# Reordering the input-projection units of a two-layer hybrid encoder: convolution units between query, key and value units

## The reference

```
h = rms_norm(x); q_a,k_a,v_a, q_r,k_r,v_r,g_r, z,xbc,dt = split(h @ w_in)
ya = sliding-window attention with sinks      (8 heads, 2 KV heads, 128 keys, relative bias)
yr = retention: rotary q,k; decayed scores; state carried over chunks; group norm; silu(g_r) *
ys = Mamba-2 SSD: xbc = silu(causal_dwconv(xbc)); decayed scores and states; * silu(z); group norm
x  = x + concat(ya, yr, ys) @ w_out
u  = rms_norm(x) @ w_up; a,b = halves;  x = x + (silu(causal_dwconv(a)) * b) @ w_down
```

## Time and profile before

| | |
|---|---|
| median of 3 runs | 1386.2 us (1384.06 to 1390.82) |
| span of the profiled execution | 1380.0 us |
| time around the span, taken as median less span | 6.2 us |
| PE busy | 1343.3 us, 97% of the span |
| DVE, ACT, POOL busy | 656.8, 628.5, 575.6 us |

### The profile page before, as it was taken

The page is one execution under the profiler, slowest core; times in us unless marked ns, Lnnn a source line. Parts: engine busy times, 40 slices in busy tenths (PEclk is TensorE's granted clock), DMA queues, the critical chain, the costliest instruction groups (busy, mean ns, idle before and its releaser), DMA issues.

```text
span 1380.0 us, 21798 instructions
## 1 busy us (share of the span) xinstructions
PE 1343.3 (97%) x6226; PEld 1071.1 (78%) x6226; DVE 656.8 (48%) x935; ACT 628.5 (46%) x965; POOL 575.6 (42%) x433
## 2 busy tenths in 40 slices
PE   6999999999999999999999999999999999999995
PEld 4787777778888888888877777777778888888884
DVE  7864567456444203443276555763754440144423
ACT  6431267166766423333362223743676662233333
POOL 3433334144554444554444333332544445444443
PEclk9999999999999999999999999999999999999998
DMA  6322122123333332333322221221323333333332
GB/s 194 100 62 62 53 70 77 39 69 92 93 105 100 99 99 84 95 103 94 106 78 76 62 62 52 59 76 45 100 78 105 98 91 107 93 90 100 98 94 105
DMA packets 65656, 119.47 MB, mean 87 GB/s; under 512 B 7320, under 2 KB 8632, under 8 KB 65464
## 3 DMA queue, kind: packets, MB, share of 16 engines
q1 hardware_dynamic: 65592, 118.64, 29.8%
HBM read 116.12 MB, written 2.49 MB: 86 GB/s over the span
## 4 chain that ended last, share of the span: by engine, by line
PE 82%; DVE 10%; issue 4%; ACT 3%; DVEq 0%; DMA 0%; ACTq 0%; SPq 0%
PE dense L894 71%; PE mix L894 10%; DVE arena L647 2%; DVE h_lo L572 1%; DVE ssq L578 1%; ACT w_hi L382 1%; PE mix L1067 1%; DVE arena L669 0%; DVE arena L840 0%; DVE arena L842 0%; DVE pad L637 0%; DVE arena L644 0%; DVE arena L885 0%; PE mix L993 0%; DVE x L628 0%
## 5 line engine op out<-in xcount | busy, mean ns | idle before, releaser
L323 POOL TENSOR_TENSOR w_lo<-w_raw,w_hi 128x512 fp32r<-128x512 f32 x428 | 575.2, 1360 | 794.0 <-ACT w_hi L382 777.4
L894 PE MATMUL dense<-h_hi,w_hi 128*128 128x512 f32 x1152 | 457.5, 397 | 13.8 <-ACT w_hi L369 6.6
L894 PE MATMUL dense<-h_lo,w_hi 128*128 128x512 f32 x1152 | 450.4, 391 | 0.0
L382 ACT ACTIVATE w_hi<-w_raw 128x512 fp32r<-128x512 f32 x424 | 249.6, 622 | 191.7 <-PE dense L894 185.5
L894 PE MATMUL dense<-h_hi,w_lo 128*128 128x512 f32 x1152 | 309.6, 391 | 0.0
L894 PEld LDWEIGHTS dense<-h_hi,w_hi 128*128 128x128 f32 x1152 | 217.3, 189 | 65.9 <-issue 13.0
L894 PEld LDWEIGHTS dense<-h_lo,w_hi 128*128 128x128 f32 x1152 | 217.3, 189 | 46.5 <-issue 2.4
L894 PEld LDWEIGHTS dense<-h_hi,w_lo 128*128 128x128 f32 x1152 | 217.4, 189 | 45.6
L894 PE MATMUL dense<-m_hi,w_hi 128*128 128x512 f32 x544 | 217.4, 400 | 3.2 <-ACT w_hi L382 2.5
L894 PE MATMUL dense<-m_lo,w_hi 128*128 128x512 f32 x544 | 212.0, 390 | 0.0
L894 PE MATMUL dense<-m_hi,w_lo 128*128 128x512 f32 x544 | 146.9, 389 | 0.0
(11 more groups left out here) (165 smaller groups left out, 1039.1 us busy)
## 6 DMA issues: line engine op xcount, KB each, us to landing
w_raw<-in_w SPq DMA_DIRECT2D x428, 256.0 KB, 2.7
x<-in_xT SPq DMA_DIRECT2D x8, 256.0 KB, 5.7
out_y<-arena SPq DMA_DIRECT2D x8, 256.0 KB, 2.1
consts<-in_consts SPq DMA_DIRECT2D x1, 1283.0 KB
rel_scratch<-arena SPq DMA_DIRECT2D x1, 382.0 KB
bias<-rel_scratch SPq DMA_DIRECT2D x8, 32.0 KB, 2.1
params<-in_params SPq DMA_DIRECT2D x1, 154.5 KB, 2.3
wdt_raw<-in_wdt SPq DMA_DIRECT2D x1, 64.0 KB
```

The costliest lines, as they stand in the source:

```text
L323: nc.gpsimd.tensor_tensor(w_lo[:, s, :], w_raw[:, s, :], w_hi[:, s, :].bitcast(f32), ALU.subtract).then_inc(lo_ready, 1)
L382: nc.scalar.activation(w_hi[:, slot, :], w_raw[:, slot, :], ACT.Copy).then_inc(hi_ready, 1)
L894: return T.matmul(dst, lhsT, rhs, start=start, stop=stop)
```

## The change

Units 0 to 11 get another meaning. Before, the convolution units are 0, 1, 3, 4, 6, 7, with K at 2, V at 5, and Q at 8 to 11. Now convolution units are 0, 2, 4, 6, 8, 10, K is 1, V is 9, and Q is 3, 5, 7, 11. The weight stream is laid out to match. In `SCHEDULE`, TOK and SA0 move back (SA0 from behind D9 to behind D12), most SSD and attention steps move back by one to three units, RV0 moves ahead of SA3, and RN0 moves from behind D35 to behind D36, while the units themselves end at D51 as before. `vtok` gets 8 KB per partition of its own, and the program's dynamic DMA scratch is set to 1024.

```diff
-U_CONV, U_K, U_V, U_Q, U_RK, U_RQ, U_RV = (0, 1, 3, 4, 6, 7), 2, 5, 8, 12, 14, 16
+U_CONV, U_Q, U_K, U_V, U_RK, U_RQ, U_RV = (0, 2, 4, 6, 8, 10), (3, 5, 7, 11), 1, 9, 12, 14, 16
 SCHEDULE = (
-    "D0 NORM D1 DT D2 DTB D3 D4 DTC D5 D6 DTD D7 D8 TOK D9 SA0 D10 D11 SB0 SA1 D12 D13 SB1 SA2 D14 D15 "
-    "SB2 SA3 D16 D17 SB3 RV0 AS0 D18 RV1 AX0 D19 RV2 AT0 AS1 D20 RV3 AX1 AV0 D21 AT1 AS2 D22 AX2 AV1 "
-    "SN0 D23 SX0 AT2 AS3 D24 AX3 AV2 SN1 D25 SX1 D26 AT3 RP0 D27 AV3 RP1 D28 RP2 D29 RP3 D30 RA0 D31 "
-    "RB0 RA1 D32 RB1 RA2 D33 RB2 RA3 D34 RB3 D35 RN0 D36 D37 RX0 D38 RX1 D39 RN1 D40 D41 RX2 D42 RX3 "
+    "D0 NORM D1 DT D2 DTB D3 D4 DTC D5 D6 DTD D7 D8 D9 TOK D10 D11 D12 SA0 D13 SB0 SA1 D14 D15 SB1 SA2 D16 D17 "
+    "SB2 RV0 SA3 D18 RV1 D19 RV2 SB3 AS0 D20 RV3 AX0 D21 AT0 AS1 D22 AX1 AV0 SN0 D23 SX0 AT1 AS2 D24 AX2 AV1 "
+    "SN1 D25 SX1 AT2 AS3 D26 AX3 AV2 D27 AT3 RP0 D28 AV3 RP1 D29 RP2 D30 RP3 D31 RA0 D32 RB0 RA1 D33 RB1 RA2 "
+    "D34 RB2 RA3 D35 RB3 D36 RN0 D37 D38 RX0 D39 RX1 RN1 D40 D41 RX2 D42 RX3 D43 D44 D45 D46 D47 D48 D49 D50 D51"
 ).split()
+_a = lay("vtok", _a, 8 * KB)
-lay("vtok", OFF["xdec"][0], 8 * KB)
-                        row = pad[:, n % 2, 3:3 + S]
+                        turn = U_CONV.index(n) % 2 if n in U_CONV else n % 2
+                        row = pad[:, turn, 3:3 + S]
-    nc = bacc.Bacc("TRN2", target_bir_lowering=False, num_devices=1)
+    nc = bacc.Bacc("TRN2", target_bir_lowering=False, num_devices=1, dynamic_dma_scratch_size=1024)
```

More of the change, by code:

```diff
@@ L162 @@
 lay("fg", 2560, S)
-assert OFF["vtok"][1] <= OFF["hst"][0]
 def build(nc, a, out):
@@ L620, in _ @@
                             dst = av[:, CH:]
-                        elif n < U_RK:
-                            t = n - U_Q
+                        elif n in U_Q:
+                            t = U_Q.index(n)
                             dst = aq[:, :, CH * t:CH * t + CH]
@@ L631, in _ @@
                             continue
-                        if U_Q <= n < U_RK:
+                        if n in U_Q:
                             V.tensor_tensor(dst, d[:, :].rearrange("p (c q) -> p c q", q=CH),
@@ L647, in _ @@
                                 ins = V.scalar_tensor_tensor(
-                                    dst, pad[:, n % 2, k:k + S], taps[:, bass.ds(l * 30 + t * 5 + k, 1)],
+                                    dst, pad[:, turn, k:k + S], taps[:, bass.ds(l * 30 + t * 5 + k, 1)],
                                     dst, ALU.mult, ALU.add)
@@ L1228, in weight_stream @@
     aq, ak, av, rq, rk, rv, rg, sz, sx = 0, 512, 640, 768, 1024, 1280, 1792, 2304, 2816
[L1229 to L1232, removed]
+    q = [np.concatenate([np.arange(aq + 64 * t, aq + 64 * t + 64),
+                         np.arange(aq + 256 + 64 * t, aq + 320 + 64 * t)]) for t in range(4)]
+    conv = [np.arange(c, c + P) for c in (sx + 512, sx + 640, sx, sx + P, sx + 2 * P, sx + 3 * P)]
+    first = {n: c for n, c in zip(U_CONV + U_Q, conv + q)}
+    first[U_K], first[U_V] = np.arange(ak, ak + P), np.arange(av, av + P)
+    cols = [first[n] for n in range(U_RK)]
     rest = [rk, rk + P, rq, rq + P] + [rv + P * t for t in range(4)]
```

## The result

The changed kernel takes 1397.79 us, the median of four runs (1396.17 to 1401.53); the kernel before took 1388.43 us beside it (1384.06 to 1390.82). The ratio is 1.0086, with a 95% interval from 1.0055 to 1.0117. The change makes the kernel slower by 0.9%, some 12 us. The two medians lie 9.4 us apart, 0.7%, which is inside the interval: it reaches from 7.6 to 16.2 us.

The account below looks back on a forecast made before the run. PE was taken as the bound, busy 1343.3 of 1380.0 us. Terms -1.6 - 1.7 + 0.4 + 2.8 + 4.8 + 4.4 + 2.6 = +11.7 us gave span 1391.7, plus 6.2 made 1397.9 us; range 1387 to 1404.

Parts of the forecast that it names:

- Start of a layer: Unit 7's wait for unit 5's evacuation on DVE shrinks by 0.8 us per layer, bounds 2.3 gained to 1.9 lost.
- the third rival: Convolutions at the layer start fall wholly under POOL's bursts: 2.7 us more per layer, 1403.3 us; chance 0.06.
- SA0 and the table loads: SSD part: five more ACT table loads per layer, one in SA0, cost 0.2 us per layer, bounds 0 and 1.28.
- AT0: PE waits at AT0 for AX0's product, behind D20's silu: 1.4 us per layer, bounds 0.8 and 2.2.
- AT3: PE waits at AT3 for AX3, queued behind SX1 on DVE: 2.4 us per layer, bounds 0.8 and 3.2.
- Unit 42: Pack behind RN1 comes late as RN0 stands one unit later: 2.2 us more idle per layer, bounds 1.6 and 2.7.
- its clock term: Half-rate dip after unit 42's wait, less 0.4 us under D44's wait: 1.3 us per layer, bounds 0 and 1.7.
- the term of 6.2 us: Time between the profiled span of before and the median of its runs, added to the forecast span of 1391.7 us.
- the two signs: Prediction wrong if unit 42's PE idle time is as before, or the clock falls where the earlier trace doesn't announce it.
- The first: Rival: chains half as late as priced and the clock holds at unit 42; +4.5 us, 1390.7 us; chance 0.25.
- The second: Rival: unit 7 starts without a wait and later chains stay under PE's work; -6.4 us, 1379.8 us; chance 0.07.
- The fourth: Rival: the clock falls at AT3 too, 1.7 or 3.4 us more, 1399.6 to 1401.3 us; chance 0.12.

Follow-up runs that it names:

- the first experiment: Changed kernel with the old mixer order, from SB3 on exactly as in the kernel before; 1383.58 us, ratio 0.9973 to the kernel before.

## Why the prediction was right, and where it was not

The forecast was 1397.9 us and slower; 1397.79 us was measured. The waits were forecast rightly in place and size, all but one too in their releaser. That the sum came within 0.1 us of the median is luck, as the end of this section shows. Step by step:

- **Start of a layer, 0.8 us gained: right.** The idle time went from 2.34 to 0.56 + 1.03 = 1.59 us, a gain of 0.75. That it comes in two pieces I hadn't seen. On DVE in the changed kernel one convolution stands ahead of DTB:

```profile
39.91 4.15 DVE L647 SCALAR_TENSOR_TENSOR arena<-pad,params,arena 128x512 f32<-128x512 f32 x3
43.97 0.41 DVE L663 TENSOR_SCALAR arena<-arena 8x512 f32<-8x512 f32 x1
...
48.78 0.69 DVE L633 TENSOR_TENSOR arena<-dense,rstd 128x512 f32<-128x512 f32 x1
...
51.56 3.35 DVE L647 SCALAR_TENSOR_TENSOR arena<-pad,params,arena 128x512 f32<-128x512 f32 x3
...
61.00 0.69 DVE L633 TENSOR_TENSOR arena<-dense,rstd 128x512 f32<-128x512 f32 x1
```

  The evacuation at 48.78, of unit 3, is late now, which gives unit 5 its 0.56 us, and leaves 1.03 us for the one at 61.00 to cost. The three L647 took 4.15 and 3.35 us, as in the earlier trace rows, so the third rival, with whole POOL bursts, fell. The window at 0.50 behind unit 7 of layer 1 went, as forecast, but one of the same length stood 20 us behind that unit, at 762.2.
- **SA0 and the table loads, 0.2 us: the lower bound, nothing.** No wait stands at SB0.
- **AT0, 1.4 us: right,** 1.24, released by L783 as foreseen, and because of D20's silu, as the experiment with AX0 shows. The lower bound was worked out wrongly: 1.4 - 0.81 is 0.6, not 0.8.
- **AT3, 2.4 us: right in size,** 2.40. The releaser is not L783 but AV2's L792 behind it. DVE shows it:

```profile
225.47 1.38 DVE L595 TENSOR_TENSOR m_lo<-arena,m_hi 128x512 fp32r<-128x512 f32 x2 [0.93 <-ACT m_hi L391]
226.77 1.27 DVE L759 SCALAR_TENSOR_TENSOR arena<-mix,bias 128x512 f32<-128x512 f32 x2
...
234.37 2.03 DVE L783 TENSOR_TENSOR arena<-arena,den 128x1024 f32<-128x1024 f32 x1
236.32 0.74 DVE L792 TENSOR_TENSOR m_lo<-mix,m_hi 128x256 fp32r<-128x256 f32 x2
```

  AX3 ended at 236.40, 9.63 us after AS3's first operation, against 9.64 in the earlier trace rows; L792 added 0.66. PE, which would have come at 237.12 - 2.40 = 234.72, was 7.87 us behind SX1's end at 226.85, where I had 237.7 - 230.48 = 7.22. The two errors of 0.65 us cancelled, which is luck. The lower bound of 0.8 doesn't follow from its two conditions either: 2.4 - 0.81 - 1.28 is 0.3.
- **Unit 42, 2.2 us: right,** 3.51 - 1.24 = 2.27. The chain was the one named. ACT:

```profile
299.08 0.63 ACT L391 ACTIVATE m_hi<-arena 128x512 fp32r<-128x512 f32 x1 [2.67 <-DVE arena L842]
299.73 1.28 ACT L499 ACT_TABLE_LOAD   x1
...
302.31 1.28 ACT L503 ACT_TABLE_LOAD   x1
...
304.66 1.14 ACT L381 ACTIVATE w_hi<-w_raw 128x512 fp32r<-128x512 f32 x2
```

  299.73 to 304.66 is again 4.93 us with two table loads. The Trainium skill, ScalarE: Activation LUTs, section What ACT_TABLE_LOAD costs, adds a drain of 1.38 us to each switch. This trace has no room for it: less the two loads, 2.37 us are left for four activations, and two drains alone would be 2.76. That the cause is the unit by which RN0 moved back fits all experiments (with RN0 behind D35 again unit 42 waits 1.24 us, and moving RX or RN1 leaves 2.15 or 2.88 us of the wait at other units), but no run moved RN0 alone.
- **Unit 44** gave back 0.35 us per layer that I had put into its clock term.

**What was mis-sized** is the term of 6.2 us that was added as time around the span, and with it the clock. An execution's own time is 1.8 us above its span (1401.53 - 1399.7, and 1.7 to 1.9 in all others). The other 4.4 us lay inside the span: the profiled execution of before, at a mean clock of 0.995, was at the fast end. Of 50 later executions of the same kernel none had a shorter span; the five at a mean clock of 0.994 had spans from 1380.0 to 1380.7 us, the eight at 0.989 from 1388.0 to 1389.3. So a base of 1386.2 us was right, but for another reason.

The clock of the changed kernel I had priced at -1.7 + 2.6 = +0.9 us, with windows at 0.50 behind unit 42 alone. In its profiled execution it was +9.3 us: 0.50 stood there, but also near 762 and for 10.2 us near 830, which the trace of before doesn't announce. That was one of the two signs that the prediction itself named for being wrong, so its account of the clock failed. Over all executions the size is open: the change costs 7.6 to 16.2 us, idle time is 9.7 of it, and the clock may be anything from 2 us gained to 6.5 us lost. Idle time had been forecast at 10.8 us, 1.1 too much. So the idle time supports the forecast, and the last digits of the sum do not.

**The rivals.** The first, with chains half as late, fell: AT3 and unit 42 cost what the forecast said, 4.8 and 4.5 us, and the clock did fall at unit 42. Its 1390.7 us lies below every execution of the changed kernel. The second, on the other side, fell with the first experiment: the start's gain is real, but 1.5 us in all, and the waits behind it are 11 us. The fourth, in which the clock falls at AT3 too, didn't occur: 2.40 us of idle time there left it alone in both layers.

**What stays open:** why the clock fell near 830. It stood at 0.50 there for 10.2 us in the profiles of the changed kernel, of AS3 ahead of SX1 and of RX0 one unit earlier, for 3.4 us near there in two others (AX0 behind AS0, RN1 later), and not at all in three: with RV0 moved, but also in two that have RV0 where the changed kernel has it. Each is one execution, so RV0's place is not shown to be the cause.

## What to carry to other kernels

When an engine is 97% busy, a reordering is worth what it does to the few chains with no slack: list for each consumer when it will be reached and when its producer ends, and after taking a wait away look at the next meeting of the same two engines, since AT0's wait came back at AT2 and unit 42's at units 43 and 44. A step that waits for another engine must not be put ahead of work that doesn't. Before a profiled span is used as a base, compare its own time and its mean clock with those of the other runs; what looks like time around the span can be a profiled execution that was lucky with its clock. And half rate is priced by the time that the engine was busy under it, not by the length of the window.

## What the runs showed of the hardware

- The granted clock varies between executions with an unchanged order of instructions: 3.4 us at 0.50 in one, 17.0 us in another, spans 1380.0 and 1388.1 us. Inside the layers 0.50 stood for 3.4, 6.8 or 10.2 us.
- At the program's start PE waited 0.56 us for DVE in eight profiles and 2.65 us in five. These five alone had 0.50 between 19.9 and 27 us.
- Idle time of 3.5 us at unit 42 came with 0.50 in both layers of the changed kernel and of that with AS3 first, in one layer with RV0 moved, and in none with AX0 first. 3.8 us at AT2, with AV ahead of AX, came with it in both layers. 2.40 us at AT3 never did, in five kernels, nor did the 2.88 us in two pieces.
- In the changed kernel the clock also fell where PE was hardly idle: near 762, behind a stretch of small matmuls with 0.39 us idle, and near 830, behind SB2 with 0.70 us idle.
- Idle time and half rate account for the spans. Take from the span of a profile PE's idle time and half of the time that PE was busy at 0.50: the thirteen profiles, with spans from 1371.0 to 1399.7 us, all leave 1350 to 1353 us.
